# A fused attention and mixture-of-experts layer on one core: expert blocks of 32 tokens over four column groups instead of 64 tokens over two

## The reference

```python
logits = xf @ router_w + router_b                 # 32 experts
top_vals, top_idx = lax.top_k(logits, 4); gates = softmax(top_vals)
# for each expert e, on the tokens routed to it:
h = x @ w1[e] + b1[e]                             # 1024 -> 2048
g, u = split(h);  g = min(g, 7);  u = clip(u, -7, 7)
act = g * sigmoid(1.702 * g) * (u + 1)
y = act @ w2[e] + b2[e]                           # 1024 -> 1024
out[token] += gate * y
```

## Time and profile before

| | |
|---|---|
| time, median of 3 runs | 3151.41 us (3151.17 to 3155.13) |
| the profiled execution's own time | 3155.27 us |
| its span in the trace | 3153.3 us |
| TensorE busy | 2825.6 us (90%) |
| VectorE, ScalarE, GpSimd busy | 707.0, 392.8, 278.8 us |
| mean granted TensorE clock | 0.941 of full speed |
| moved by DMA | 504.08 MB, mean 160 GB/s |

### The profile page before, as it was taken

How to read it: one execution, slowest core, us unless ns; L and a number is a source line. 1 busy time by engine, 2 the same in 40 slices (tenths; PEclk the granted TensorE clock), 3 DMA queues, 4 the chain that set the end, 5 groups by cost and what they waited for, 6 DMA issues and landing times.

```text
span 3153.3 us, 32994 instructions
## 1 busy us (share of the span) xinstructions
PE 2825.6 (90%) x12166; PEld 1171.7 (37%) x12167; DVE 707.0 (22%) x1741; ACT 392.8 (12%) x824; POOL 278.8 (9%) x367
## 2 busy tenths in 40 slices
PE   8999997999989679899999799899799979975575
PEld 4645565444445223233333233233233323321121
DVE  4334776011133211111111111111111111110012
ACT  2002553000013000000000000000000000000002
POOL 0000000000001211011111011011111111110000
PEclk9998898999999789899999899899899989987787
DMA  3100002200053586513553737553866664487773
GB/s 128 53 27 0 1 1 76 84 21 25 9 185 119 195 320 221 192 27 132 180 190 87 290 90 279 201 184 129 338 233 213 242 250 163 150 330 307 303 291 127
DMA packets 139364, 504.08 MB, mean 160 GB/s; under 512 B 26912, under 2 KB 44704, under 8 KB 106304
## 3 DMA queue, kind: packets, MB, share of 16 engines
q1 hardware_dynamic: 106176, 460.22, 37.8%
q0 software_dynamic: 19536, 43.10, 6.6%
q10 hardware_dynamic: 13600, 0.10, 0.2%
HBM read 469.06 MB, written 34.64 MB: 160 GB/s over the span
## 4 chain that ended last, share of the span: by engine, by line
PE 58%; DMA 11%; SPq 1%; DVE 1%; issue 1%; POOL 0%; DVEq 0%; ACT 0%; ACTq 0%; POOLq 0%
PE xbank L1252 32%; PE xbank L1275 18%; DMA w_hi<-in_w 9%; PE xbank L1206 3%; PE xbank L1242 1%; PE xbank L1262 1%; PE xbank L1234 1%; DMA reg_r<-in_w 1%; PE xbank L1269 1%; PE xbank L1192 0%; SPq L860 0%; DVE reg_h L1168 0%; DMA w_hi<-in_b 0%; POOL slot_rows L884 0%; SPq L856 0%
## 5 line engine op out<-in xcount | busy, mean ns | idle before, releaser
L1252 PE MATMUL xbank<-reg_r,stage 128*64 128x512 f32 x2592 | 597.0, 615 | 197.0 <-DMA reg_r<-in_w 196.3
L1252 PE MATMUL xbank<-w_hi,stage 128*64 128x512 f32 x2592 | 572.5, 593 | 9.6 <-DMA w_hi<-in_w 9.6
L1275 PE MATMUL xbank<-reg_r,stage 128*64 128x512 f32 x2592 | 572.4, 594 | 2.4 <-DVE stage L1149 2.4
L1252 PEld LDWEIGHTS xbank<-reg_r,stage 128*64 128x64 f32 x2592 | 190.9, 142 | 591.3 <-issue 586.1
L1275 PEld LDWEIGHTS xbank<-reg_r,stage 128*64 128x64 f32 x2592 | 182.6, 137 | 363.6 <-issue 354.7
L1252 PEld LDWEIGHTS xbank<-w_hi,stage 128*64 128x64 f32 x2592 | 181.0, 137 | 355.2 <-issue 319.7
L531 PE MATMUL pair<-reg_r,reg_h 128*128 128x512 f32 (+1 forms) x640 | 252.7, 550 | 0.3 <-DMA reg_r<-in_w_in 0.3
L1149 DVE COPY stage<-xbank 128x512 f32<-128x512 f32 x81 | 56.0, 691 | 792.6 <-PE xbank L1242 788.3
L1138 DVE TENSOR_SCALAR stage<-xbank 128x512 f32<-128x512 f32 x81 | 56.0, 692 | 620.3 <-PE xbank L1252 620.3
L902 POOL TENSOR_TENSOR idxs<-idxa,tok 128x1 int32<-128x1 int32 x81 | 15.2, 188 | 1677.2 <-ACT stage L979 1677.2
L531 PEld LDWEIGHTS pair<-reg_r,reg_h 128*128 128x128 f32 x640 | 119.2, 191 | 114.2 <-issue 110.1
(11 more groups left out here) (187 smaller groups left out, 2031.4 us busy)
## 6 DMA issues: line engine op xcount, KB each, us to landing
reg_r<-in_w SPq DMA_DIRECT2D x64, 2048.0 KB, 12.6
w_hi<-in_w SPq DMA_DIRECT2D x64, 2048.0 KB
reg_r<-in_w SPq DMA_DIRECT2D x128, 1024.0 KB, 7.3
reg_r<-in_w_in SPq DMA_DIRECT2D x4, 2048.0 KB, 7.8
reg_r<-in_x SPq DMA_DIRECT2D x8, 512.0 KB, 3.5
reg_ka<-in_w_in SPq DMA_DIRECT2D x8, 512.0 KB, 3.9
reg_g<-in_w_in SPq DMA_DIRECT2D x8, 512.0 KB, 3.9
reg_r<-in_w_o SPq DMA_DIRECT2D x1, 4096.0 KB, 17.0
```

Source lines behind the costliest of these rows:

```text
L1252: ins = pe.matmul(up_bank[b][h][QB * c:QB * c + QB, :], xT[b][:, k % HG, QB * (k // HG):QB * (k // HG) + QB], w1k[k][:, h * FF + c * FG:h ...
L1275: ins = pe.matmul(y_bank[b][QB * j:QB * j + QB, 0:DG], actT[:, k % HG, QB * (k // HG):QB * (k // HG) + QB], w2r[:, k, j * DG:(j + 1) * DG] ...
```

## The change

- QB goes from 64 to 32 and NG, the number of column groups, from 2 to 4. DG and FG, the columns that a group has of a row of x or y and of each half of w1, go from 512 to 256.
- In `up`, a matmul's moving side is 2 x 256 columns (the same columns of both halves), so one PSUM bank takes a block: 8 x 4 = 32 matmuls of 512 moving columns, 64 records, with a stationary side of 128 x 32. In `down` there are 8 x 4 = 32 matmuls of 256 moving columns, 64 records.
- x and the activation are turned by VectorE's transpose of 32x32 squares, straight from SBUF to SBUF. The transposes on TensorE and their two copies go. `turn_x(n+2)` stands on VectorE after `swiglu(n)`.
- The squares leave the contraction in another order, so the rows of w1 and w2 are loaded in that order: partition 32j + q of piece k of w1 holds row 256j + 32k + q.
- w1 is loaded in eight transfers of 1 MB, each released by its own k; w2 in four of 1 MB as before, now with 8 KB to a partition in one run (before 2 runs of 4 KB).
- Each block has four loads of slots instead of two. Tables, waits and constants follow the sizes.

```diff
-QB = 64
+QB = 32
 NG = P // QB
-NPAD = 104
+NPAD = 168
-W1P, W2P = 4, 4
+W1P, W2P = 8, 4
-        w1_d = a["w1"][0].rearrange("e (q k p) n -> e q p k n", p=P, k=2)
-        w2_d = a["w2"][0].rearrange("e (q k p) n -> e q p k n", p=P, k=2)
+        w1_d = a["w1"][0].rearrange("e (j k q) n -> e k j q n", j=NG, q=QB)
+        w2_d = a["w2"][0].rearrange("e (j h q k) n -> e h j q (k n)", j=NG, h=W2P, q=QB)
...
                 for q in range(W1P):
                     sp.wait_ge(w1_used[q], ended)
-                    sp.dma_start(w1q[q], w1_d[bass.ds(i + 1, 1), q].rearrange("o p k n -> (o p) k n")).then_inc(w1_in[q], 16)
+                    sp.dma_start(w1k[q], w1_d[bass.ds(i + 1, 1), q].rearrange("o j q n -> (o j) q n")).then_inc(w1_in[q], 16)
...
                 if reused:
-                    pool.wait_ge(x_turned, n - 1)
+                    pool.wait_ge(xT_ready, n - 1)
...
             def swiglu(n, b):
...
-                dve.tensor_tensor(act_s, ul, sg, ALU.mult).then_inc(act_ready, 1)
+                dve.tensor_tensor(act_s.rearrange("p (h k q) -> p h q k", h=W2P, k=2), ul.rearrange("p (h q k) -> p h q k", h=W2P, k=2),
+                                  sg.rearrange("p (h q k) -> p h q k", h=W2P, k=2), ALU.mult)
+                dve.drain()
+                dve.transpose(actT[b], act_s).then_inc(act_ready, 1)
+
+            def turn_x(n, b, half):
+                dve.wait_ge(xg_in[b], half * 16 + 16)
+                if not isinstance(n, int) or n >= 2:
+                    dve.wait_ge(up_done, n - 1)
+                dve.transpose(xT[b], xg[b]).then_inc(xT_ready, 1)
...
             with dve.Fori(0, PAIRS) as i:
                 with dve.If(i < n_iters):
                     for m in range(2):
                         n = i * 2 + (m + 1)
-                        store_act(i * 2 + m)
                         swiglu(n, 1 - m)
+                        turn_x(n + 2, 1 - m, i + (m + 1))
                         dve.wait_ge(y_done, n)
                         choose(n + 1, m)
...
             def up(b, loaded, ks):
                 for k in ks:
-                    if k % 2 == 0:
-                        pe.wait_ge(w1_in[k // 2], loaded)
-                    for h in range(2):
-                        for c in range(NG):
-                            ins = pe.matmul(up_bank[b][h][QB * c:QB * c + QB, :], xT[b][:, k % HG, QB * (k // HG):QB * (k // HG) + QB],
-                                            w1k[k][:, h * FF + c * FG:h * FF + (c + 1) * FG], start=(k == 0), stop=(k == KD - 1))
-                    if k % 2 == 1:
-                        ins.then_inc(w1_used[k // 2], 1)
+                    pe.wait_ge(w1_in[k], loaded)
+                    for c in range(NG):
+                        ins = pe.matmul(up_bank[b][QB * c:QB * c + QB, :].rearrange("p (h f) -> p h f", h=2),
+                                        xT[b][:, QB * k:QB * k + QB],
+                                        w1k[k].rearrange("p (h f) -> p h f", h=2)[:, :, c * FG:(c + 1) * FG],
+                                        start=(k == 0), stop=(k == KD - 1))
+                    ins.then_inc(w1_used[k], 1)
...
                         up(b, loaded[m + 1], range(0, 4))
-                        turn_act(i * 2 + m)
-                        turn_x(n + 1, m, i + 1)
                         up_bias(n, b)
                         up(b, loaded[m + 1], range(4, 8))
                         down(i * 2 + m, m, loaded[m])
```

More of the change, by code:

```diff
@@ L725, in expert_half @@
         w1k = [w1_half[k // 4][:, k % 4, :] for k in range(KD)]
-        w1q = [w1_half[q // 2][:, 2 * (q % 2):2 * (q % 2) + 2, :] for q in range(W1P)]
         w2r = reg_r[:, 8192:16384].rearrange("p (k n) -> p k n", k=KD)
+        w2q = [reg_r[:, 8192 + q * 2 * D:8192 + (q + 1) * 2 * D] for q in range(W2P)]
         stage = sb("stage", [P, 6 * D])
@@ L761, in expert_half @@
         xg = [stage[:, n * DG:(n + 1) * DG] for n in range(2)]
-        xT = [stage[:, D + n * DG:D + (n + 1) * DG].rearrange("p (h s) -> p h s", h=HG) for n in range(2)]
+        xT = [stage[:, D + n * DG:D + (n + 1) * DG] for n in range(2)]
         gl, ul, sg = (stage[:, 2 * D + n * FG:2 * D + (n + 1) * FG] for n in range(3))
-        act_s = stage[:, 3 * D + FG:4 * D]
-        actT = stage[:, 4 * D:4 * D + FG].rearrange("p (h s) -> p h s", h=HG)
-        yrow = [stage[:, 4 * D + FG + n * DG:4 * D + FG + (n + 1) * DG] for n in range(2)]
+        act_s = stage[:, 3 * D:3 * D + FG]
+        actT = [stage[:, 3 * D + (n + 1) * FG:3 * D + (n + 2) * FG] for n in range(2)]
+        yrow = [stage[:, 4 * D + n * DG:4 * D + (n + 1) * DG] for n in range(2)]
         sel = [sb(f"sel{n}", [96, QB], BF16) for n in range(2)]
@@ L800, in expert_half @@
         idxg_ready, idxs_ready = sem("idxg_ready"), sem("idxs_ready")
-        x_turned, xT_ready, act_turned, actT_taken = (sem(n) for n in ("x_turned", "xT_ready", "act_turned", "actT_taken"))
+        xT_ready = sem("xT_ready")
         gate_min, up_taken, sig_ready, act_ready, sel_ready = (sem(n) for n in ("gate_min", "up_taken", "sig_ready", "act_ready", "sel_ready"))
@@ L956, in load_slots @@
                 if not (isinstance(half, int) and half == 0):
-                    act.wait_ge(idx_in[b], half * (16 * NG))
+                    act.wait_ge(idx_in[b], half * 64)
                 row = act.value_load(listi[0:1, 1, bass.ds(n, 1)], min_val=0, max_val=TABROWS - QB)
@@ L1228, in _ @@
             pe.matmul(bank[2][0:96, 128:128 + NPAD], ones_f[0:32, 0:96], past[:, :], start=True, stop=True).then_inc(blocks_done, 1)
[L1230 to L1243, removed]
@@ L1257, in up_bias @@
+                    ins.then_inc(w1_used[k], 1)
             def up_bias(n, b):
                 pe.wait_ge(sel_ready, n + 1)
-                for h in range(2):
-                    for c in range(NG):
-                        pe.matmul(up_bank[b][h][QB * c:QB * c + QB, :], sel[b][:, :],
-                                  b1p[:, h * FF + c * FG:h * FF + (c + 1) * FG], start=False, stop=False)
+                for c in range(NG):
+                    pe.matmul(up_bank[b][QB * c:QB * c + QB, :].rearrange("p (h f) -> p h f", h=2), sel[b][:, :],
+                              b1p[:, :].rearrange("p (h f) -> p h f", h=2)[:, :, c * FG:(c + 1) * FG], start=False, stop=False)
@@ L1274, in down @@
                     for j in range(NG):
-                        ins = pe.matmul(y_bank[b][QB * j:QB * j + QB, 0:DG], actT[:, k % HG, QB * (k // HG):QB * (k // HG) + QB],
+                        ins = pe.matmul(y_bank[b][QB * j:QB * j + QB, 0:DG], actT[b][:, QB * k:QB * k + QB],
                                         w2r[:, k, j * DG:(j + 1) * DG], start=False, stop=(k == KD - 1))
```

42 lines of the change are left out of this document (14 added, 28 removed).

## The result

| | before | changed |
|---|---|---|
| time, median | 3153.27 us (3151.17 to 3156.42) | 6207.7 us (6202.05 to 6232.09) |
| ratio to before, 95% interval | | 1.97 [1.9642, 1.9758] |
| span in the trace | 3153.3 us | 6200.2 us |
| TensorE busy | 2825.6 us | 2986.5 us |
| mean granted TensorE clock | 0.941 | 0.689 |

The change makes the kernel nearly twice as slow. The forecast was 3092 us with a range up to 3270, so size and sign were both wrong.

What follows compares the result with a forecast made beforehand. It took TensorE to bound the kernel, and weight loads in one-block experts. From 1061.5, 25.8 + 443 + 1425 + 47 us ended at 3002; 50 for clock and 10 for slots made 3062, a gain of 59: 3092 us, range 2985 to 3270.

Steps and rivals of the forecast that it cites:

- the flow of the weights: Weight loads at a change of expert: 8 of 12 pieces in 22.7 us (taken as 22.0), 33 us of flow an expert.
- rival 3: Weight loads flow slower from the rows' layout in HBM; at 20% slower the time is 3255 us; chance 0.12.
- The 4 MB rule: Skill's statement on weight-like copies: half the rate where partitions' rows lie 4 MB apart, full rate at 512 KB.
- A block of 10.8 us: TensorE's up and down for one 32-token block, four column groups at once: 10.8 us.
- Rivals 1 and 2: Four column groups not together: 21.4 us blocks, about 4280 us, chance 0.12; or partly: 13.3 us, 3380 us, 0.06.
- 248 us less work on TensorE: Expert stage's blocks: 145 x 10.8 = 1566 us against 1814 before, a gain of 248 us.
- 7.8 us at a change of a long expert: TensorE's wait for the next w1 at each expert with 3 blocks or more: 7.8 us.
- the forecast's 10 us for slots and gathers: Slots, gathers and tail: gathers on GpSimd just fit, but under load not always; 10 us in all.
- 36.9 us for an expert of one or two blocks: Load-bound experts with 1 or 2 blocks: 33 us of flow and 3.9 us of gap, 36.9 us each.
- 1.6 for the clock: Lower granted TensorE clock at each of 31 changes of expert: 1.6 us, between ends 0 and 3.5; 50 us.
- rival 4: Gather chain over GpSimd binds, adding 1 us to each block of the long experts: 3211 us; chance 0.12.
- Rival 5: Clock stays up during waits and the weight loads flow at 410 GB/s: 2996 us; chance 0.15.

Runs made afterwards that it cites:

- e4: Kernel before, with only the sources of both weights' transfers changed to four runs of rows (4 outermost): 6348.62 us, 2.0136.
- e1: Changed kernel, each weight transfer reading 128 rows in one run, with three bounded count reads at the loop's turn: 3278.04 us, 1.0395.
- e2: Changed kernel, same addresses and row order, each 1 MB piece issued as four transfers of 32 rows: 4058.61 us, 1.2879.
- e11: Changed kernel with row 8p + k in partition p, each 1 MB piece as four transfers to 32 neighbouring partitions each: 4032.62 us.
- e9: Changed kernel without the loads of experts 1 to 31, all blocks using expert 0's weights: 2693.7 us, 0.8547.
- e10: Kernel before without the loads of experts 1 to 31, all blocks using expert 0's weights: 2924.08 us, 0.9278.
- e7: Changed kernel with row 8p + k in partition p (128 outermost) and TensorE's bounded reads of the load counts spread over the turn: 3207.07 us, 1.0163.
- e8: Kernel before with w1 in eight 1 MB transfers, rows in line, each released by its own k, count reads spread: 3129.24 us, 0.992.

## Why the prediction was wrong

**The step that failed** is the flow of the weights, "8 of 12 pieces take 34 x 8/12 = 22.7 us" and "33 us of flow". It carried the 385 GB/s of the earlier trace rows over to sources of another shape. They flow at 103 to 106: one expert takes 119 us. e4 and e1 show from both sides that this alone makes the factor of two. I did ask whether the new layout was slower (rival 3), but only for its addresses, and priced it up to 20%; the cause, the number of engines, was in no case, so the range was cut at 3270. A row could have raised the question: a load's rate is share times engines, and in the trace before it was 0.99 x 16 engines x 24 GB/s. Nothing there says what fills the 16.

The Trainium skill does say it, on a page that the prediction cites for something else: "DMA: Bandwidth & Descriptors", section "Why a DMA increments its semaphore by 16 and not by 1". A transfer from this queue uses the largest number up to 16 that divides the slowest dimension above size 1 of source and destination. By that rule j = 4 gives 4 engines; the shares 0.13, 0.25, 0.51 and 1.03 agree at every size tried. The 4 MB rule that I weighed in its place was the wrong one: the runs lie 2 MB apart, each of the four engines at work kept its full 26.5 GB/s over them, and e2 and e11 differ in the jumps and not in the rate.

Point by point:

- **A block of 10.8 us: right.** 10.65 us in the changed kernel and in e9, four groups at once. Rivals 1 and 2 are refuted, and with them, for this kernel, the 2.38x for three column tiles that the prediction quotes. Only the turn of the loop was overlooked, 0.46 us of issue and 0.2 in the up behind it for two blocks.
- **248 us less work on TensorE: right**, 270 in the expert stage by e10 minus e9; 22 of it come from 10.65 instead of 10.8.
- **7.8 us at a change of a long expert: mis-sized**, even with healthy loads. The change of expert read in e7 costs 13.8 us, and the mean of eleven is 15.0. The last piece came 27.0 us after the last up began, not 25.0, and the last records of the first up behind it ran at a granted clock of 0.50 (8 records in 1.93 us, where 32 take 3.44). w2 was not in time within 1 us: the second down took 5.6 us (1612.5 to 1618.1) instead of 3.46, with w2's last piece late. Eighteen of them by 15.0 - 9.4 = 5.6 us more are 101 us, and the turns of the loop 72 x 0.3 = 22, against 18 saved by 10.65 for 10.8: with 3092 that makes 3197, where e7 has 3207. (The sum keeps the forecast's 10 us for slots and gathers, of which e7 shows 3.)
- **36.9 us for an expert of one or two blocks, 1.6 for the clock: right** where the loads are healthy. From the end of the first up of such an expert to that of the next, the twelve take 38.8 us on average in e7.
- **Gathers, VectorE, rival 4: next to no effect.** In e9 TensorE is busy 100.00 of 100 us, and in e7 it waits 3.0 us in all for a transpose of x. VectorE's transposes of 128x256 take 0.42 us each in the changed kernel, the lower of the two ends that I gave.
- **Rival 5** fell with the loads: 0.50 in the waits.

The rows below are those groups of VectorE in the changed kernel. Even the multiply that writes in permuted order, 0.62 us, is covered.

```profile
L1142 DVE STREAM_TRANSPOSE stage<-stage 128x256 f32<-128x256 f32 x147 | 61.2, 417 | 242.3 <-DMA stage<-xn_rows,idxg 242.3
L1132 DVE TENSOR_TENSOR stage<-stage 128x256 f32<-128x256 f32 x145 | 90.1, 622 | 10.8
```

So two errors of one kind. The work on TensorE was worked out from rows and held. What a faster block uncovers was under-priced twice: by the shape of the transfer, and, once that is healed, by the stall at each change of expert, which, with the turns of the loop, is enough to turn a gain of 270 us in the stage into a loss of 50.

## What to carry to other kernels

When an edit rearranges the source or the destination of a transfer, look first at its outermost dimension and at the partitions it covers, before its addresses: keep the 128 partitions outermost, in one transfer. In a profile, read rate and DMA share together: a low share in a stretch that waits for a transfer (0.25 at 106 GB/s here) meant too few engines, a full share at a low rate (1.02 at 222 GB/s in e11) meant engines that hindered each other. And where weights are held once, halving the time of a block uncovers their load; price that at every change before counting the gain, since here finer pieces alone (e8) gave 24 us, 0.8% and clear of the interval, and the whole change, healed, lost 54.

## What the hardware showed that I had not expected

- A transfer with an outermost dimension of 4 ran at 103 to 106 GB/s with a DMA share of 0.25, while each engine at work kept its 26.5 GB/s; other transfers in the same queue did not fill the idle ones.
- All 16 engines writing 32 neighbouring partitions moved 222 GB/s, and a packet of 8 KB took 0.59 us; writing every fourth partition, 401 GB/s and 0.32 us, with transfers of the same size.
- 64 KB between the rows of neighbouring partitions cost nothing: 416 against 417 GB/s.
- Three bounded reads of a register at the start of a turn held TensorE for 1.54 to 1.57 us; one there and two in the middle of an up, for 0.10 to 0.17.
